# State-space output in head pairs, and the norms around the second block's output projection in smaller pieces

## The reference, cut to what matters

```
def ssd_branch(z, xbc, dt_raw, ...):
    xbc = silu(causal_dwconv(xbc, conv_w) + conv_b)      # xs 1024, B and C 4 groups x 128
    y = ssd_chunked(xs, dt, A, B, C)                     # 16 heads of 64, per head: (CB * decay) @ (x*dt)
    y = y + D_skip[:, None] * xs
    return group_rmsnorm(y * silu(z), norm_g, 4)         # 4 groups of 256 channels
def short_conv_branch(gate_b, gate_c, h, conv_w, norm_g):
    v = causal_dwconv(gate_c * h, conv_w)                # 3 taps
    return group_rmsnorm(gate_b * v, norm_g, 16)         # 16 groups of 64 channels
```

## Time and profile before

| | |
|---|---|
| median of 3 runs | 1773.28 us (1772.43 to 1775.71) |
| the profiled execution | 1773.51 us, of which the profile's span is 1771.7 us |
| mean granted TensorE clock | 0.984 |
| second half of the input projection, with the scan | about 1219 to 1348 us of the span |
| output projection | about 1356 to 1428 us |

### The profile page before, as it was taken

The page is one execution under the profiler, slowest core; times in us unless marked ns, Lnnn a source line. Parts: engine busy times, 40 slices in busy tenths (PEclk is TensorE's granted clock), DMA queues, the critical chain, the costliest instruction groups (busy, mean ns, idle before and its releaser), DMA issues.

```text
span 1771.7 us, 25327 instructions
## 1 busy us (share of the span) xinstructions
PE 1694.1 (96%) x10482; PEld 1362.2 (77%) x10482; DVE 1036.1 (58%) x1512; ACT 835.5 (47%) x1202; POOL 0.9 (0%) x5
## 2 busy tenths in 40 slices
PE   8989999999999999998898999999998999999996
PEld 5736566777877786897688999899876968777775
DVE  3426655544334444435666566658666658888885
ACT  3434543533222323423646454555444437766764
POOL 0000000000000000000000000000000000000000
PEclk9989999999999999999999999999998999999998
DMA  9212623244334425223024454344222419899992
GB/s 392 98 53 96 211 98 145 75 187 157 118 141 166 168 82 190 72 98 117 1 73 166 159 204 146 137 164 145 96 96 72 143 53 378 339 335 342 355 326 105
DMA packets 42822, 287.76 MB, mean 162 GB/s; under 512 B 4800, under 2 KB 5952, under 8 KB 11600
## 3 DMA queue, kind: packets, MB, share of 16 engines
q1 hardware_dynamic: 42528, 285.97, 44.2%
q10 hardware_dynamic: 144, 0.06, 0.0%
q0 software_dynamic: 32, 0.07, 0.0%
HBM read 285.03 MB, written 1.05 MB: 161 GB/s over the span
## 4 chain that ended last, share of the span: by engine, by line
PE 85%; DVE 8%; ACT 4%; issue 2%; DMA 1%; DVEq 0%; ACTq 0%; SPq 0%
PE ps L512 17%; PE ps L514 16%; PE ps L513 16%; PE ps L2743 5%; DVE WL L497 3%; PE ps L2713 2%; PE ps L2717 2%; PE ps L2714 2%; PE ps L557 2%; PE ps L1429 1%; PE ps L1527 1%; PE ps L1498 1%; PE ps L537 1%; PE ps L675 1%; PE ps L2619 1%
## 5 line engine op out<-in xcount | busy, mean ns | idle before, releaser
L512 PE MATMUL ps<-HH,WH 128*128 128x512 f32 (+2 forms) x1488 | 495.7, 333 | 16.8 <-DVE WL L497 6.8
L497 DVE TENSOR_TENSOR WL<-ring,WH 128x2048 fp32r<-128x2048 f32 (+2 forms) x192 | 413.5, 2160 | 147.1 <-ACT WH L487 146.8
L514 PE MATMUL ps<-HH,WL 128*128 128x512 f32 (+2 forms) x1488 | 483.7, 325 | 0.0
L513 PE MATMUL ps<-HL,WH 128*128 128x512 f32 (+2 forms) x1488 | 483.2, 325 | 0.0
L487 ACT ACTIVATE WH<-ring 128x2048 fp32r<-128x2048 f32 (+2 forms) x192 | 346.9, 1809 | 196.4 <-PE ps L514 77.1
L512 PEld LDWEIGHTS ps<-HH,WH 128*128 128x128 f32 x1488 | 284.3, 191 | 68.3 <-issue 33.3
L514 PEld LDWEIGHTS ps<-HH,WL 128*128 128x128 f32 x1488 | 284.2, 191 | 21.7
L513 PEld LDWEIGHTS ps<-HL,WH 128*128 128x128 f32 x1488 | 284.7, 191 | 20.1 <-issue 0.2
L512 PE MATMUL ps<-parts,WH 128*128 128x512 f32 (+1 forms) x352 | 119.7, 340 | 0.0
L513 PE MATMUL ps<-parts,WH 128*128 128x512 f32 (+1 forms) x352 | 118.4, 336 | 0.0
L514 PE MATMUL ps<-parts,WL 128*128 128x512 f32 (+1 forms) x352 | 118.3, 336 | 0.0
(11 more groups left out here) (357 smaller groups left out, 2258.8 us busy)
## 6 DMA issues: line engine op xcount, KB each, us to landing
ring<-wts SPq DMA_DIRECT2D x196, 1024.0 KB, 5.0
arena<-wts SPq DMA_DIRECT2D x46, 1024.0 KB, 6.6
ring<-wts SPq DMA_DIRECT2D x32, 704.0 KB, 4.0
ring<-wts SPq DMA_DIRECT2D x4, 672.0 KB, 13.5
X<-xin SPq DMA_DIRECT2D x4, 512.0 KB, 16.3
cst<-csts SPq DMA_DIRECT2D x1, 1373.0 KB, 20.6
ring<-wts SPq DMA_DIRECT2D x3, 384.0 KB, 3.8
out<-arena SPq DMA_DIRECT2D x2, 512.0 KB, 2.9
```

The costliest lines, as they stand in the source:

```text
L497: e.tensor_tensor(lo, raw(i), hi.bitcast(F32), ALU.subtract).then_inc(*up("low", i))
L512: e.matmul(o, w[0][:, cols], x[0], start=k == 0, stop=False)
L513: e.matmul(o, w[0][:, cols], x[1], start=False, stop=False)
L514: return e.matmul(o, w[1][:, cols], x[0], start=False, stop=k == nk - 1)
```

## The change

1. **Head pairs.** `pe_head_out` does nothing for an even head. For an odd one it does both heads of the pair, alternating: first part of head h-1, of h, second part of h-1, of h, and so on. Even heads write output columns 0 to 63, odd ones 64 to 127. A fourth EE buffer lies in constants that are no longer used (`cst` from `r128` on), and waits on `head_out` go back four heads instead of three.
2. **Sums on quarters.** The group sums and the sums of short-convolution tiles 6 and 7 are made in four column groups of 32, each with a quarter of the tokens (68): `pe_quarters`. So root and inverse work on 128 x 68 instead of 4 or 16 x 272, and each spread takes four (L2494) or eight (L2161) matmuls of 68 tokens. Sums of tiles 0 to 5 stay as they were.
3. **Norm tile by tile.** The spread and scaling of tiles 0 to 2 move to step 21, those of 3 to 5 stay in step 22; on VectorE the low part of a tile follows the scaling of the next.
4. **Output projection.** k = 0 to 5 of chunk 0, last group sum and last sum, k = 0 to 5 of chunk 1, spread of tiles 6 and 7, then k = 6, 7 of both chunks, then the spreads of groups 0 and 1. The group norm's root and inverse come before those of tiles 6 and 7.

The core of the diff (the widened constants `strip` and `strip4`, and the plain renaming of EE, are left out):

```diff
+        def pe_quarters(e, b, strip, x, start, stop):
+            q = NT // 4
+            for g in range(4):
+                t = e.matmul(ps[32 * g:32 * g + 32, b, 0:q], strip, x[:, q * g:q * g + q], start=start, stop=stop)
+            return t
...
+                if of:
+                    q = NT // 4
+                    for g in range(4):
+                        for h in range(2):
+                            c = 32 * g + 2 * (x - of) + h
+                            t = e.matmul(ps[64 * h:64 * h + 64, b, q * g:q * g + q], ident[:, c:c + 1].to_broadcast([128, 64]),
+                                         sc_quarter, start=True, stop=True)
...
+            def low(x):
+                e.wait_ge(*at("yc_high", x))
+                e.tensor_tensor(YP[1][:, 8 + x, :], YC[:, x, :], YP[0][:, 8 + x, :].bitcast(F32),
+                                ALU.subtract).then_inc(*up("yc_low", x))
...
-                e.wait_ge(*at("yc_high", x))
-                e.tensor_tensor(YP[1][:, 8 + x, :], YC[:, x, :], YP[0][:, 8 + x, :].bitcast(F32),
-                                ALU.subtract).then_inc(*up("yc_low", x))
+                if x > first:
+                    low(x - 1)
+            low(last)
...
+            for c, o, a, n in ((0, 0, 0, 272), (1, 16, 272, 256), (2, 144, 528, 128)):
+                for i in pair:
+                    r = 64 * (i % 2)
+                    t = e.matmul(ps[r:r + 64, b, o:o + n], XD[0:TLEN[c], c, 64 * i:64 * i + 64],
+                                 EE[i % 4][0:TLEN[c], a:a + n], start=c == 0, stop=c == 2)
...
-            if f == 22:
-                pe_sc_norm(e, 0, 5)
+            if f in (21, 22):
+                pe_sc_norm(e, 3 * f - 63, 3 * f - 61, 0)
...
+                    if half and i < 2:
+
+                        pe_wout_tiles(e, half, i, early)
+                        if i == 0:
+                            pe_group_sum(e, 7)
+                            pe_sc_sum(e, 7, 6, 7)
+                            continue
+                        pe_sc_norm(e, 6, 7, 6)
+                        for n in range(2):
+                            pe_wout_tiles(e, half, n, late)
```

More of the change, by code:

```diff
@@ L2302, in pe_group_sum @@
             e.wait_ge(*at("y_square", x))
[L2303 to L2304 removed]
+            t = pe_quarters(e, banks.of["group_sums",], C("strip4")[:, 3 - g:35 - g], XC[:, x, :], x == 0, x == 7)
             if x == 7:
@@ new lines, in pe_wout @@
+                    weights(e, index["wout", half, i])
+                    for m in range(2):
+                        bank(e, "wout", half, 2 * i + m)
+                    if half and i < 2:
[7 more added lines that the diff above has]
+                            pe_wout_tiles(e, half, n, late)
+                    else:
+                        pe_wout_tiles(e, half, i, [(m, k) for m in range(2) for k in range(8)])
@@ L2441, in pe_wout @@
+                    for n in range(2) if half and i == 1 else (i,):
+                        for m in range(2):
+                            banks.give(banks.of["wout", half, 2 * n + m], "mixed", half, 2 * n + m)
+                        if half:
+                            pe_group_spread(e, n)
+                    if not half:
                         for j in (2 * i, 2 * i + 1):
@@ L2447, in pe_wout, with pe_group_spread @@
             pe_warm(e, b, 3, HH)
+        def pe_group_spread(e, i):
+            b = bank(e, "spread.group", i)
+            e.wait_ge(*at("inverse.group"))
+            q = NT // 4
+            for g in range(4):
+                t = e.matmul(ps[:, b, q * g:q * g + q], ident[:, 32 * g + i:32 * g + i + 1].to_broadcast([128, 128]), sd_root,
+                             start=True, stop=True)
+            t.then_inc(*up("spread.group", i))
+            banks.give(b, "ys_unit", 2 * i + 1)
         def act_wout(e):
```

164 lines of the change are left out of this document (80 added, 84 removed).

## The result

| | before | after |
|---|---|---|
| median of the runs | 1773.18 us (1772.43 to 1775.71, 4 runs) | 1761.01 us (1759.84 to 1761.54, 4 runs) |
| profiled execution, and its span | 1773.51, 1771.7 us | 1759.84, 1758.0 us |
| mean granted TensorE clock | 0.984 | 0.987 |

The ratio is 0.9926, 95% interval 0.9912 to 0.9941: 13.1 us less on 1773.2 (10.5 to 15.6), 12.2 by the medians. I had said 7.9 us less and the range ended at 1760.5; by the ratio the kernel now takes about 1760.1 us, and by the medians it is 4.4 us better than forecast. The sign was right, the size was not.

What follows compares the result with a forecast made beforehand. TensorE was taken as the bound, busy without a break through the scan, with VectorE as brake once TensorE got faster. Terms -10.0 - 2.3 - 0.6 + 5.0 = -7.9 us gave 1765.4 us, range 1760.5 to 1769.5.

Steps and rivals of the forecast that it cites:

- Pairs on TensorE: In the scan, two heads' outputs side by side cost 1.59 us, as much as one: TensorE gains 12.7 us.
- rival 2: In the scan, a pair's halves run one after another, a pair costing 2.7 us: total 1766.7 us, chance 0.05.
- VectorE brakes: In the scan, VectorE can drop only 7.4 us of idle time, 6.1 before heads' first operations; 25.0 us for exponentials stay.
- Rival 3: VectorE does not brake, since its waits for ScalarE shrink too: the whole 17 us, 1758.4 us, chance 0.04.
- The first output matmul, -10.0: The output projection's first matmul starts 10.0 us earlier: 7.4 from VectorE's idle time, 2.6 from the quicker norm.
- Tiles 0 to 2 in step 21 cost nothing of their own: In the scan, the norm of these tiles lies in a TensorE wait, so moving it counts as nothing.
- First output matmul to chunk 2, 23.2: In the output projection, 15.1 us of work plus waits 2.2, 1.2 and 4.7: 23.2 us against 25.5, gain 2.3.
- Group spreads, -0.6: For groups 2 and 3, the spread loses its change of geometry, 0.3 us each: gain 0.6.
- The clock, +5.0: Half-clock stretches, chiefly behind the new wait before chunk 2, cost 5.0 us; bounds 1.7 and 6.7.
- Rival 1: The clock falls only behind idle time, not narrow matmuls: 1.7 us replace 5.0, total 1762.1 us, chance 0.12.
- My list of signs: Profile signs, including TensorE waits in the scan's last third; wrong if the scan shows 0.50 or chunk 2's wait is missing.
- rival 4: Slower: the clock falls in the scan itself, a third of it at 0.50 giving about 1779 us, chance 0.03.

Runs made afterwards that it cites:

- e7: Changed kernel with a pair's six matmuls ordered head by head instead of alternating: first output matmul 5.5 us later, median 1766.1 us.
- e1: Kernel before the change plus only the head pairs and fourth EE buffer: first output matmul 8.0 us earlier, stretch 9.8 us shorter, median 1766.0 us.
- e3: Changed kernel with each tile's subtraction right behind its own scaling: first output matmul 2.4 us later, chunk 2 3.5 us later, median 1765.7 us.
- e13: Changed kernel with the norm of all six tiles in step 22: first output matmul 1.6 us later, router 2.3 us later, median 1762.8 us.
- e5: Changed kernel with the feed-forward statistics' bank taken ahead of the output projection again: first output matmul 0.9 us later, chunk 2 unmoved, median 1761.9 us.
- e2: Changed kernel with each head's three matmuls in its own step again: first output matmul 6.1 us later, router 5.4 us later, median 1765.8 us.
- e8: Changed kernel with the spread of tiles 6 and 7 inside chunk 0 again: chunk 2 0.4 us later, router 1.1 us earlier, median 1761.9 us.
- e12: Changed kernel with group sums, root, inverse and spread undivided on 272 columns: first output matmul 0.1 us later, router 0.4 us earlier, median 1764.4 us.
- e6: Changed kernel with 16 unread full-width matmuls filling the wait before chunk 2: chunk 2 takes 6.96 us, not 8.37, router 1.5 us earlier, median 1762.2 us.
- e14: Changed kernel with seven unread wide matmuls before the spreads of tiles 0 and 2: first output matmul at 91.14 us against 91.16, median 1761.6 us.
- e9: Changed kernel with chunk 2's and chunk 1's weights split earlier, groups' low parts one tile behind, two group spreads moved: median 1755.8 us, ratio 0.9889 to before.

## Why the prediction was right in sign and wrong in size

- **Pairs on TensorE**: right. 1.60 us a pair against 1.59; rival 2 (no overlap) gives what e7 shows when the order is undone on purpose, 2.97 us where I had worked out 2.7.
- **VectorE brakes**: right. Its removable 6.1 us are gone, its 25 us of waits for ScalarE stayed, e1 gained 8.0 us of 12.7 at the first output matmul (7.4 expected), and taking the pairs out costs only 5.4. Rival 3 falls. That TensorE would wait in the last third of the scan: three waits, 3.0 us, all behind 1330 us; the slack besides is spent in a half-clock stretch, 6.8 us long.
- **The first output matmul, -10.0: the step that failed second.** It came 11.6 us earlier. The norm's low part one tile behind was right (2.6; e3 shows 2.4). "Tiles 0 to 2 in step 21 cost nothing of their own" puts this part at nothing; with all six tiles in step 22 (e13) the first output matmul comes 1.6 us later and chunk 2 1.5, the size of the miss. How much of that is a clock stretch twice as long isn't known. I also let the first matmul wait for the sixth scaling as before; the changed kernel starts it 0.25 us behind the fifth, which is worth at most 0.9 us there and nothing at chunk 2 (e5). These figures overlap, as do the two gains in e1 and e2, and don't add up.
- **First output matmul to chunk 2, 23.2**: right as a sum (23.3) and in its parts. Waits 2.2, 1.2 and 4.7 were foreseen; the trace has 1.7 (0.3 + 1.4), 1.1 and 4.2. What I credited to putting both chunks ahead of the spread is worth nothing (e8).
- **Group spreads, -0.6**: wrong. Chunk 3 to the router grew by 0.2 us, and e12's single spread is the cheaper one.
- **The clock, +5.0: the step that failed first.** "I take 5.0, since the stretch behind the new wait has nothing beside it." The place was right and nothing is beside it (e6: without the low clock the router comes 1.5 us earlier), but I took the size from a stretch of 10 us at 0.50. Behind the new wait 0.50 lasted 3.4 us and cost 1.5 us. That is below my lower bound of 1.7, and it isn't a constant of this wait: behind the same 4.2 us in e5, e7 and e13 it lasted 6.8 us, with chunk 2 at 9.2 to 9.7 us instead of 8.4, so 2.2 to 2.7 us. The other stretch, in the scan, is longer, and in the changed kernel e14 shows half of it to cost nothing. 3.5 us of the 4.2 us missed are this term.

I had also misread where 0.50 began in the kernel before. The earlier trace rows show it from 1356.0 us, and I put it behind the 2.1 us wait; but the windows between show that it began ahead of that wait, while TensorE was busy (the 0.66 is the mean of a window that begins at 1.00 and ends at 0.50):

```profile
1352.00:1354.00 2.00, 1.94 (x7) 0.45 (x5) 1.28 (x4) 0.62 (x2) 0.00 (x0) 0.66 0.00 0
1354.00:1356.00 2.00, 0.00 (x0) 0.01 (x1) 1.27 (x4) 0.63 (x2) 0.00 (x0) 0.50 0.00 0
```

It was granted from 1352.66 to 1359.5 us, 6.8 us, behind the narrow matmuls of the last scan step and with no wait of TensorE ahead of it since 1248 us. So the kernel before has a half-clock stretch at the end of its scan too, as long as the one that the changed kernel has from 1332.5.

Rival 1 names nearly the right number, 1.7 us, for a wrong reason. The Trainium skill (TensorE: Matmul & The Clock Gate, section Why this matters for your kernels) has the clock fall behind long idle gaps; but 0.50 was granted from 1332.5 us, where the longest wait so far had been 1.1 us (to 1332.67), and in the kernel before with no wait at all. My list of signs said that 0.50 in the scan would prove the prediction wrong. It was there, at the scan's end, and rival 4's price did not follow, because VectorE was the later engine.

What stays open: how the 1.6 us of e13 divide between banks and clock, the price of the bank order alone, what started the half-clock stretch in the scan (narrow matmuls and short waits lie together there; e2 and e7, the changed kernel with its pairs not side by side, don't have it, but the kernel before, without pairs too, does), and why the same wait is followed by 3.4 us at 0.50 in some kernels and 6.8 in others.

## What to carry to other kernels

Charge a lowered clock only where TensorE is the engine that ends last, by the length of stretch that such a wait shows in several places, and with both ends kept in the range; the largest stretch in the trace is a bound, not a value. Look for the start of a half-clock stretch in windows without gaps before naming what it stands behind. A speed-up of the bound engine stops where the second engine's idle time for its sake is used up: read that idle time line by line, and add what each other edit takes off the second engine, since it comes on top. When a new wait can be named in advance ("4.7 us for chunk 2's weights, behind the first group's normalizing"), it can also be edited away at once: moving that split ahead of the normalizing was worth 4.5 us, more than a third of the whole change.

## What the runs showed of the hardware

- Two products in different 64-column halves overlapped in alternation and hardly at all one behind the other: twelve matmuls 1.60 us alternating, 2.97 us head by head, and 3.18 us in two separate steps. The Trainium skill (TensorE: Matmul & The Clock Gate, section Why this matters for your kernels) gives small output tiles in distinct column groups as running together; the trace agrees for neighbours in the program (both start at 1273.68), and shows that the order must bring them there.
- The same code reached the first exponential at 1251.20 us in one profile (e8) and at 1255.78 in another (e9). Ahead of it 0.50 was granted for 20.5 us in all in e8 and in e1 (1251.35), 23.9 in after (1252.38) and e12 (1252.47), 27.3 in before and most others (1253.1 to 1255.0) and 30.7 in e3, e6, e9 (1255.4 to 1255.8): from the first to the last about 1.4 us for each 3.4 us more at half clock. That goes with most of the scatter of the profiles ahead of the change, and it is why single microseconds were read between fixed instructions.
- A table load took 1.28 us, and the activation behind it started 1.29 us after the load's start (1252.38 to 1253.67); nothing more was paid for the change of tables.
